# The edge between two rounds of a chunked RWKV-7 scan, written in another order on four queues

## The chip, the cores and the metric

The kernel runs on one core of one Trainium2 chip. The metric is the device time of one execution in microseconds (us), the median of several. A core has a matrix engine (TensorE, PE in the profile; its weight loads are PEld), a vector engine (VectorE, DVE), an activation engine (ScalarE, ACT), GpSimd (POOL) and SyncE (SP), which issues the transfers. Each works through its own queue in order and waits on semaphores for the others.

## The reference

Two encoder layers over 512 tokens of width 1024. Each mixes tokens in two groups side by side, latent attention and a bidirectional RWKV-7 scan of 8 heads, projects the result out, and ends in a gated MLP with a convolution. The change concerns the RWKV group alone:

```python
h = rms_norm(x) * (1 + sc1) + sh1
z_rwkv = centred_token_shift((h @ w_in[l])[..., MLA_IN:], rwkv_mu[l])
def step(state, inp):                      # wkv7_scan: 512 tokens, forward and reversed
    sa = jnp.einsum('bhvk,bhk->bhv', state, -kk_t)
    state = (state * w_t[:, :, None, :] + sa[..., None] * (kk_t * a_t)[:, :, None, :]
             + v_t[..., None] * k_t[:, :, None, :])
    y = jnp.einsum('bhvk,bhk->bhv', state, r_t)
...
y = y_f + y_b                              # rwkv7_group: 8 heads of 64
y = ((y - mu) * lax.rsqrt(var + GN_EPS)).reshape(B, S, W) * gn_g + gn_b
return (y + bonus.reshape(B, S, W)) * g
...
x = x + gt1 * (jnp.concatenate([y_mla, y_rwkv], axis=-1) @ w_out[l])
x = x + gt2 * conv_ffn(rms_norm(x) * (1 + sc2) + sh2, ...)
```

## The kernel before

**Stages.** A layer runs the input projection, the latent attention, the RWKV stage, the output projection, and the MLP. In the profiled execution the RWKV stage of the first layer stands at about 285 to 558 us and that of the second at about 1251 to 1535 us. This stage uses hardly any transfers.

**Blocks and rounds.** RW is 512 channels, or four blocks of 128 (two heads `e` each), and both directions `d` are worked on together. The 512 tokens of a block are cut into 8 chunks of 64. `rwkv_round(l, cur, nxt)` is called for `cur` = -1, 0, 1, 2, 3 (PE line 801). In one round the engines scan block `cur` in eight steps `s`, build what block `nxt = cur + 1` needs, and finish block `cur - 1` (`trail`). Round -1 only builds; round 3 only scans and finishes. What a reader sees as "the edge" is the stretch between the last step of one round and the first solve of the next.

**One step of the scan.** `scan_state` (L614, L618, L620) multiplies by the carried state, `scan_solve` (L627) multiplies by the inverse of the chunk's triangle, `scan_update` (L637 for the next state, L643 for the output) closes the step. Between them stand the products for later chunks: `scan_gram` for `s + 2` (L577), `scan_values` for `s + 1` (L599) and the transposes `scan_tokens` for `s + 2` (L589, L591, L592). VectorE masks each Gram pair into one of two buffers `GR` (L1419, "the mask") and scales the state (L1425, "the state product"). ScalarE moves R (L975), the token transposes (L970) and the solution (L982) out of the banks. A step can't begin its solve before the state product of the step before it.

**The build of the next block.** VectorE sums the decays (L1283), makes the queries of a direction (L1290 to L1296), its removals (L1301, L1304) and its keys (L1309, L1311); these need ScalarE's exponentials `grown` (Pp, L917) and `shrunk` (Pi, L921) and the factor f (L926). TensorE makes the triangles (L524), ScalarE moves them (L938), VectorE transposes them into lanes (`inverse_in`, L1342) and inverts them by rows of 8, 16 and 32 (L1348 to L1406), then transposes the result back (`inverse_out`, L1414, "out"). The bonus is made by L1315, L1317, a product on TensorE (L532) and L1322.

**The level.** At the edge TensorE turns the 32 by 32 inverses into 64 by 64 ones: 32 transposes X (L543), 32 products T (L548) and 32 products Z (L556). ScalarE evicts each half (L952, L957, L964) and copies the two diagonals (`diagonal`, L945, two operations each). After the level TensorE issues Gram pair 1, values 0 and tokens 1, and then the first solve. Before the level stand the early products of the block after next (`rwkv_early`, L509, in banks 5 and 6), with ScalarE's `early_decay` and `early_rate` (L905, L907, L912) and a reversed copy of the values (L931), and Gram pair 0 and tokens 0.

**The tail of a block.** ScalarE takes the output of the scan (L989), TensorE centres it at step 3 (L650) and sums its squares at step 5 (L655), ScalarE takes a logarithm and an exponential, each with a table load (L999, L1001), TensorE multiplies by the gate (L657), and VectorE finishes the norm (`tail_norm`, L1432 to L1436) at step 6.

**What sets the order.** The order on each queue is the order of the calls in the `rwkv_round` of that engine (PE, ACT and DVE have one each), written by hand. `at(name, round)` and `before(name, round)` turn the name of a step into the count of a semaphore.

## Time and profile before

| | us |
|---|---|
| three timed runs | 1986.78, 1987.35, 1992.8 |
| their median | 1987.35 |
| the profiled execution's own time | 1992.84 |
| its span | 1990.9 |
| PE busy | 1706.3 (86%) |
| DVE busy | 1072.9 (54%) |
| ACT busy | 720.6 (36%) |
| POOL busy | 292.1 (15%) |

The profiled execution lies at the upper end of the three timed runs; 1.94 us of it lie outside the span. Over the whole span TensorE is busy 86% of the time, but this is an average over dense projections and the RWKV stage, where the four queues wait for each other in turn. Rows of the timeline give start, duration, engine, line, operation and operands, and in square brackets the idle time of that engine just before and what ended it.

### The profile page before, as it was taken

To read this page: it belongs to the slowest core of one execution; us is meant where nothing else is said; L and a number is where in the kernel's file an instruction comes from. 1 tells how busy PE (TensorE), PEld (TensorE's weight loads), DVE (VectorE), ACT (ScalarE), POOL (GpSimd) and SP (SyncE) were. 2 spreads that over 40 slices of the span, in tenths; PEclk is the share of its full clock that TensorE was granted. 3 is DMA by queue.
4 is the path that set the end of the run, shared out by engine and by line. 5 is a ranking of instruction groups with operands and counts; after the bars stand their busy time and mean duration, and the time that the engine had idled before them with its cause. 6 is when DMAs were issued, how large, how long until landed. Compare 5 with 4: busy or idle time off the path is not lost.

```text
span 1990.9 us, 27789 instructions
## 1 busy us (share of the span) xinstructions
PE 1706.3 (86%) x11192; PEld 1262.2 (63%) x11192; DVE 1072.9 (54%) x1533; ACT 720.6 (36%) x1160; POOL 292.1 (15%) x124
## 2 busy tenths in 40 slices
PE   2996855888877999999989988488888989999997
PEld 1783424656654888878858734266665668888785
DVE  6744558777344767663343343876773155454433
ACT  3433243445424232322243343434544232322322
POOL 0440000000022121211124400000000212221220
PEclk8998875788788999999999989576777989999999
DMA  7443110000032555542303300000001212223222
GB/s 275 169 158 112 43 59 1 2 2 2 2 144 89 187 192 180 199 148 85 116 23 117 108 29 1 0 2 2 1 2 43 85 64 86 104 84 105 85 87 82
DMA packets 34651, 162.96 MB, mean 82 GB/s; under 512 B 3840, under 2 KB 4096, under 8 KB 25856
## 3 DMA queue, kind: packets, MB, share of 16 engines
q1 hardware_dynamic: 34560, 161.65, 23.3%
q8 instruction: 69, 1.13, 0.2%
q14 instruction: 22, 0.18, 0.0%
HBM read 159.54 MB, written 2.10 MB: 81 GB/s over the span
## 4 chain that ended last, share of the span: by engine, by line
PE 71%; DVE 17%; ACT 6%; issue 5%; DMA 1%; POOL 0%; DVEq 0%; SPq 0%; ACTq 0%; POOLq 0%
PE bank L487 12%; PE bank L489 12%; PE bank L488 12%; PE bank_pair L487 4%; PE bank_pair L489 4%; PE bank_pair L488 4%; DVE work L1336 3%; PE bank L774 2%; PE bank L775 2%; PE bank L556 1%; PE bank_pair L577 1%; PE bank L548 1%; DVE work L1395 1%; PE bank L752 1%; PE bank L704 1%
## 5 line engine op out<-in xcount | busy, mean ns | idle before, releaser
L487 PE MATMUL bank<-work_parts,y_mix_parts 128*128 128x512 f32 x792 | 316.1, 399 | 24.3 <-DVE work_parts L1499 16.0
L489 PE MATMUL bank<-work_parts 128*128 128x512 f32 x792 | 314.9, 398 | 0.0
L1512 DVE TENSOR_TENSOR work_parts<-work,y_mix_parts 128x1024 fp32r<-128x1024 f32 x66 | 169.4, 2567 | 253.5 <-ACT y_mix_parts L876 253.5
L1721 POOL TENSOR_TENSOR proj_weights_parts<-proj_weights,proj_weights_hi 128x1024 fp32r<-128x1024 f32 x54 | 131.5, 2438 | 1049.8 <-ACT proj_weights_hi L870 974.1
L1726 POOL TENSOR_TENSOR work_parts<-work,y_mix_parts 128x1024 fp32r<-128x1024 f32 x66 | 160.4, 2431 | 616.8 <-ACT y_mix_parts L876 616.8
L876 ACT ACTIVATE y_mix_parts<-work 128x1024 fp32r<-128x1024 f32 x132 | 132.8, 1054 | 251.3 <-DMA work<-mlp_dram 251.3
L488 PE MATMUL bank<-work_parts,y_mix_parts 128*128 128x512 f32 x528 | 209.0, 396 | 0.0
L487 PEld LDWEIGHTS bank<-work_parts,y_mix_parts 128*128 128x128 f32 x792 | 150.2, 190 | 66.3 <-issue 24.8
L489 PEld LDWEIGHTS bank<-work_parts 128*128 128x128 f32 x792 | 150.2, 190 | 35.6
L487 PE MATMUL bank<-work_parts,proj_weights_hi 128*128 128x512 f32 x304 | 126.5, 416 | 42.1 <-DVE work_parts L1499 27.0
L489 PE MATMUL bank<-work_parts,proj_weights_parts 128*128 128x512 f32 x304 | 123.5, 406 | 0.0
L488 PEld LDWEIGHTS bank<-work_parts,y_mix_parts 128*128 128x128 f32 x528 | 100.1, 190 | 23.2
L488 PE MATMUL bank<-mixer_inputs_parts,y_mix_parts 128*128 (+1 forms) x264 | 104.5, 396 | 0.0
L489 PE MATMUL bank_pair<-work_parts 128*128 128x512 f32 x264 | 104.4, 396 | 0.0
L487 PE MATMUL bank_pair<-work_parts,y_mix_parts 128*128 128x512 f32 x264 | 104.2, 395 | 0.0
L487 PEld LDWEIGHTS bank<-work_parts,proj_weights_hi 128*128 128x128 f32 x304 | 60.1, 198 | 65.6 <-issue 36.1
L577 PE MATMUL bank_pair<-work 64*128 64x128 f32 x512 | 62.2, 349 | 31.0 <-DVE work L1419 30.4
L1215 DVE CUSTOM_DVE_ANT_0 work<-work,c_act 128x1024 f32<-128x1024 f32 x64 | 80.5, 1295 | 12.3 <-DMA work<-ada_dram 12.2
L1172 ACT ACTIVATE work<-work 128x512 f32<-128x512 f32 x44 | 27.9, 633 | 160.3 <-DVE work L1669 160.3
L488 PE MATMUL bank<-work_parts,proj_weights_hi 128*128 128x512 f32 x208 | 83.0, 399 | 0.0
L577 PEld LDWEIGHTS bank_pair<-work 64*128 64x128 f32 x512 | 47.6, 231 | 40.6 <-DVE work L1419 35.5
L509 PE MATMUL bank<-mixer_inputs 64*128 64x512 f32 x64 | 40.8, 1035 | 33.6 <-DVE y_mix L1322 13.1
(253 smaller groups left out, 3176.2 us busy)
## 6 DMA issues: line engine op xcount, KB each, us to landing
work<-mlp_dram SPq DMA_DIRECT2D x66, 1024.0 KB, 4.9
work<-ada_dram SPq DMA_DIRECT2D x64, 512.0 KB, 4.6
proj_weights<-tiles_dram SPq DMA_DIRECT2D x57, 512.0 KB, 3.5
x_res<-ada_dram SPq DMA_DIRECT2D x24, 512.0 KB, 4.9
x_res<-x_dram SPq DMA_DIRECT2D x2, 2048.0 KB, 10.6
mixer_inputs<-ada_dram SPq DMA_DIRECT2D x8, 512.0 KB, 17.5
work<-mlaw_dram SPq DMA_DIRECT2D x4, 640.0 KB, 4.3
out_dram<-x_res SPq DMA_DIRECT2D x8, 256.0 KB, 2.2
```

What stands on the lines that cost most here:

```text
L487: mm(out, w_hi, x_hi, start=start, stop=False)
L488: mm(out, w_hi, x_lo, start=False, stop=False)
L489: return mm(out, w_lo, x_hi, start=False, stop=stop)
L509: own(ear_p, mm(PS[5 + d][:, :], l_rw[rows, b, i, :], mix(x)[rows, :], start=True, stop=True), f"{n}{d}")
L577: last = mm(PS[3 + e][:, d * P:(d + 1) * P], BK[p][d][rows, s, :, :], ZR[p][d][rows, s, :, :], start=True, stop=True)
L774: mm(bank[:, :], QN[:, e, qb * P:(qb + 1) * P], KN[:, e, :], start=True, stop=False)
L876: F(MW_H[q][:, half], MW_IN[q][:, half], ACT.Identity).then_inc(msp_a.sem, msp_a.one(f"h{half}"))
L1215: dve.tensor_tensor_reduce(out=slots[u], in0=slots[u], in1=CACT, scale=0.5, scalar=0.0, op0=ALU.mult, op1=ALU.add, accum_out=dots[:, u:u + ...
L1336: return TTT(tmp, rows.unsqueeze(1).to_broadcast([64, c, a, j]), cols.unsqueeze(2).to_broadcast([64, c, a, j]), ALU.mult)
L1512: TTT(MW_L[q][:, 1], MW_IN[q][:, 1], plain(MW_H[q][:, 1]), ALU.subtract).then_inc(msp_v.sem, msp_v.one("l1"))
L1721: pool.tensor_tensor(ring_l[s], ring[s], plain(ring_h[s]), ALU.subtract).then_inc(spl_q.sem, spl_q.one(f"t{s}"))
L1726: pool.tensor_tensor(MW_L[q][:, 0], MW_IN[q][:, 0], plain(MW_H[q][:, 0]), ALU.subtract).then_inc(msp_q.sem, msp_q.one("l0"))
```

## The change

All of it is in the RWKV stage; the work is the same except where named.

- **Edge, TensorE.** Gram pair 1 goes between the transposes X and the products T, values 0 and tokens 1 between T and Z; before, all three stood behind Z. Early products and level use banks 1 and 2 in place of 5 and 6. Since bank 2 holds the output of the scan, the early products now wait until ScalarE has taken it, and until the last solution is evicted.
- **Edge, ScalarE.** The exponentials stand between the evictions of the level: Pp0 and Pp1 before the evictions of T0 and T1, Pi0 behind them, Pi1 between Z0 and Z1. Before, Pp1 and Pi1 stood behind the level. Half of the diagonal copies go to VectorE. Both factors f follow the first solve. The reversed copy of the values moves from the edge to step 4.
- **Edge, VectorE.** Queries and removals of both directions, two diagonal copies and the norm of the block two rounds back stand ahead of step 0. In the steps, each mask comes first; behind it the two key pairs at step 0, the bonus at 1, the inverse in other portions at 2 to 7.
- **Tail.** The gate product moves from step 5 to behind step 6, and the norm to the edge of the next round; in round 3 its own norm stays at step 6. The norm works in YQ.
- **Masks.** `GR` has three buffers in place of two, and a mask waits for its Gram pair only, not for the tokens behind it.

```diff
-        GR = [view(WORK, 8192 + 512 * p, 2, 2, P) for p in range(2)]
+        GR = [view(WORK, 8192, 2, 2, P), view(WORK, 8704, 2, 2, P), view(RS, 512, 2, 2, P)]
...
-                elif trail:
-                    pe.wait_ge(tl_v.sem, tl_v.at("gt", it - 3))
-                else:
-                    pe.wait_ge(tri_a.sem, tri_a.at("B11", it - 1))
-                    pe.wait_ge(bon_v.sem, bon_v.at("bon", it - 1))
+                if scan:
+                    pe.wait_ge(sc_a.sem, sc_a.at(f"SA{NCH - 1}", it - 2))
+                    pe.wait_ge(tl_a.sem, tl_a.at("y", it - 2))
...
-                        own(ear_p, mm(PS[5 + d][:, :], l_rw[rows, b, i, :], mix(x)[rows, :], start=True, stop=True), f"{n}{d}")
+                        own(ear_p, mm(PS[1 + d][:, :], l_rw[rows, b, i, :], mix(x)[rows, :], start=True, stop=True), f"{n}{d}")
...
-                if d == 0:
-                    pe.wait_ge(lev_a.sem, lev_a.before("Z1", it))
-                    pe.wait_ge(ear_a.sem, ear_a.at("A1", it))
+                if d == 0 and it % RB >= 3:
+                    pe.wait_ge(tl_v.sem, tl_v.at("gt", it - 3))
...
                 if early:
                     pe.wait_ge(ear_a.sem, ear_a.at("A1", it + 1))
-                else:
-                    pe.wait_ge(tl_v.sem, tl_v.at("gt", it - 2))
+                elif scan:
+                    pe.wait_ge(sc_a.sem, sc_a.at(f"SA{NCH - 1}", it - 1))
+                    pe.wait_ge(tl_a.sem, tl_a.at("y", it - 1))
...
                     own(lev_p, last, f"X{d}")
+                scan_gram(it, 1)
                 for d in D2:
...
                     own(lev_p, last, f"T{d}")
+                scan_values(it, 0)
+                scan_tokens(it, b, 1)
                 pe.wait_ge(lev_a.sem, lev_a.at("T1", it))
...
+                if s == 0:
+                    pe.wait_ge(inv_v.sem, inv_v.at("d1", it))
...
+                    if trail and s == 6:
+                        tail_gate(old, cur - 1)
...
-                for e in range(2):
-                    src = XD[32 * q:32 * q + 32].rearrange("p (d e c) t -> p e d c t", d=2, e=2)[:, e]
-                    own(lev_a, F(XT[it % 2][64 * e + 32 * q:64 * e + 32 * q + 32, :, :, 32 * q:32 * q + 32], src, ACT.Identity), f"D{q}{e}")
+                src = XD[32 * q:32 * q + 32].rearrange("p (d e c) t -> p e d c t", d=2, e=2)[:, 1]
+                own(lev_a, F(XT[it % 2][64 + 32 * q:96 + 32 * q, :, :, 32 * q:32 * q + 32], src, ACT.Identity), f"D{q}")
...
                     act.wait_ge(lev_p.sem, lev_p.at(f"X{d}", it))
-                    own(lev_a, F(X0T[0:32, 16 * d:16 * d + 16, :], sixteen(PS[5 + d][0:32, :]), ACT.Identity), f"X{d}")
-                if nxt < RB:
-                    grown(it + 1, 0)
+                    own(lev_a, F(X0T[0:32, 16 * d:16 * d + 16, :], sixteen(PS[1 + d][0:32, :]), ACT.Identity), f"X{d}")
                 for d in D2:
+                    if nxt < RB:
+                        grown(it + 1, d)
                     act.wait_ge(lev_p.sem, lev_p.at(f"T{d}", it))
-                    own(lev_a, F(X0T[32:64, 16 * d:16 * d + 16, :], sixteen(PS[5 + d][32:64, :]), ACT.Identity), f"T{d}")
+                    own(lev_a, F(X0T[32:64, 16 * d:16 * d + 16, :], sixteen(PS[1 + d][32:64, :]), ACT.Identity), f"T{d}")
...
-                    own(lev_a, F(XT[it % 2][rows, :, :, 32:64], PS[5 + e][rows, :].rearrange("p (d c t) -> p d c t", d=2, c=NCH), ACT.Identity), f"Z{e}")
+                    own(lev_a, F(XT[it % 2][rows, :, :, 32:64], PS[1 + e][rows, :].rearrange("p (d c t) -> p d c t", d=2, c=NCH), ACT.Identity), f"Z{e}")
+                    if e == 0 and nxt < RB:
+                        shrunk(it + 1, 1)
                 diagonal(it, 1)
...
-                act.wait_ge(tl_v.sem, tl_v.before("gt", it))
+                act.wait_ge(tl_p.sem, tl_p.before("cen", it))
...
-                if scan:
-                    scan_state(it, 0)
-                elif build:
-                    grown(new, 0)
-                    shrunk(new, 0)
-                if build:
-                    grown(new, 1)
-                    shrunk(new, 1)
+                if build and not scan:
+                    for d in D2:
+                        grown(new, d)
+                    for d in D2:
+                        shrunk(new, d)
                 for s in range(NCH):
                     if scan:
-                        if s:
-                            scan_state(it, s)
+                        scan_state(it, s)
                         if s < NCH - 1:
                             scan_ring(it, s + 1)
                         scan_solve(it, s)
+                    if build and s == 0:
+                        factor(new, nxt, 0)
+                        factor(new, nxt, 1)
                     if build and s in (0, 1):
-                        factor(new, nxt, s)
                         triangle(new, s)
+                    if build and scan and s == 4:
+                        backward_values(new, nxt)
                     if trail and s == 3:
                         tail_square(old)
...
-                    backward_values(new + 1, nxt + 1)
...
+            def diagonal(it, q):
+
+                dve.wait_ge(inv_v.sem, inv_v.at("out", it))
+                src = XD[32 * q:32 * q + 32].rearrange("p (d e c) t -> p e d c t", d=2, e=2)[:, 0]
+                own(inv_v, dve.tensor_copy(XT[it % 2][32 * q:32 * q + 32, :, :, 32 * q:32 * q + 32], src), f"d{q}")
...
-                dve.wait_ge(sc_p.sem, sc_p.at(f"K{s}" if s > 1 else f"G{s}", it))
-                own(sc_v, TTT(GR[s % 2].rearrange("p e d x -> p e (d x)"), PAIR[:, :, 0:256], gmask.unsqueeze(1).to_broadcast([P, 2, 256]), ALU.mult),
+                dve.wait_ge(sc_p.sem, sc_p.at(f"G{s}", it))
+                own(sc_v, TTT(GR[s % 3].rearrange("p e d x -> p e (d x)"), PAIR[:, :, 0:256], gmask.unsqueeze(1).to_broadcast([P, 2, 256]), ALU.mult),
...
                     queries(new, nxt, 0)
+                if scan:
+                    diagonal(it, 0)
+                    diagonal(it, 1)
+                if build:
+                    queries(new, nxt, 1)
                     removals(new, nxt, 0)
+                    removals(new, nxt, 1)
+                if cur > 1:
+                    tail_norm(old - 1, cur - 2)
                 for s in range(NCH):
-                    if build:
-                        if s == 0:
-                            queries(new, nxt, 1)
-                        if s == 1:
-                            keys(new, nxt, 0)
-                        if s == 2:
-                            bonus(new, nxt)
-                        if s == 3:
-                            inverse_8(new, 1, 7)
-                        if s == 4:
-                            bonus_end(new, nxt)
-                            inverse_16_second(new)
-                        if s == 5:
-                            inverse_32_first(new, 0)
-                        if s == 6:
-                            inverse_32_mid(new, 1)
                     if scan and s < NCH - 1:
                         scan_ring(it, s + 1)
                     if build:
                         if s == 0:
-                            removals(new, nxt, 1)
+                            keys(new, nxt, 0)
+                            keys(new, nxt, 1)
                         if s == 1:
-                            keys(new, nxt, 1)
+                            bonus(new, nxt)
                         if s == 2:
                             inverse_in(new)
+                            inverse_8(new, 1, 4)
                         if s == 3:
-                            inverse_8(new, 7, 8)
+                            inverse_8(new, 4, 8)
                             inverse_16_first(new)
                         if s == 4:
+                            bonus_end(new, nxt)
+                            inverse_16_second(new)
                             inverse_16_end(new)
                         if s == 5:
+                            inverse_32_first(new, 0)
                             inverse_32_first(new, 1)
+                        if s == 6:
                             inverse_32_mid(new, 0)
-                        if s == 6:
-                            inverse_32_second(new, 0)
-                    if trail and s == 6:
+                            inverse_32_mid(new, 1)
+                    if trail and not build and s == 6:
                         tail_norm(old, cur - 1)
                     if scan and s < NCH - 1:
                         scan_state(it, s)
                     if build and s == 7:
+                        inverse_32_second(new, 0)
                         inverse_32_second(new, 1)
```

**ScalarE at the edge** between the rounds 0 and 1 (L952/L959 evict X, L957/L964 evict T, L964/L971 evict Z, L945/L952 copy a diagonal, L917/L924 is Pp, L921/L929 is Pi, L975/L984 takes R; before, then now):

```order
L970 ACTIVATE work<-bank 128x512
L952 ACTIVATE work<-bank 32x512 x2
L917 ACTIVATE work<-work 128x512
L957 ACTIVATE work<-bank 32x512 x2
L921 ACTIVATE work<-work 128x512
L945 ACTIVATE work<-work 32x16x32 x2
L964 ACTIVATE work<-bank 32x16x32 x2
L945 ACTIVATE work<-work 32x16x32 x2
L975 ACTIVATE rstd<-bank 128x128
L917 ACTIVATE work<-work 128x512
L921 ACTIVATE work<-work 128x512
```

```order
L979 ACTIVATE work<-bank 128x512
L959 ACTIVATE work<-bank 32x512 x2
L924 ACTIVATE work<-work 128x512
L964 ACTIVATE work<-bank 32x512
L924 ACTIVATE work<-work 128x512
L964 ACTIVATE work<-bank 32x512
L929 ACTIVATE work<-work 128x512
L952 ACTIVATE work<-work 32x16x32
L971 ACTIVATE work<-bank 32x16x32
L929 ACTIVATE work<-work 128x512
L971 ACTIVATE work<-bank 32x16x32
L952 ACTIVATE work<-work 32x16x32
```

The second Pp moved from behind the R eviction into the gap of the T products, the second Pi into the gap of the Z products, and each diagonal is one copy in place of two.

**VectorE at the steps 2 and 3** of a round, from one state product to the next but one (L1419/L1433 is the mask, L1425/L1439 the state product, L1342/L1350 `inverse_in`, L1348 to L1365 the rows up to 8 and the first product of 16, L1356 to L1373 now; before, then now):

```order
L1419 TENSOR_TENSOR work<-bank_pair,constants 128x512
L1342 STREAM_TRANSPOSE work<-work 64x1024
L1425 TENSOR_TENSOR rstd<-bank,chunk_ends 128x128
L1348 COPY lane_inverse<-work 64x4
L1354 TENSOR_TENSOR work<-work,lane_inverse 64x16
...
L1356 TENSOR_REDUCE lane_inverse<-work 64x4x6
L1419 TENSOR_TENSOR work<-bank_pair,constants 128x512
L1354 TENSOR_TENSOR work<-work,lane_inverse 64x196
L1356 TENSOR_REDUCE lane_inverse<-work 64x4x7
L1336 TENSOR_TENSOR work<-work,lane_inverse 64x512 x2
L1365 TENSOR_REDUCE work<-work 64x128
L1425 TENSOR_TENSOR rstd<-bank,chunk_ends 128x128
```

```order
L1433 TENSOR_TENSOR work<-bank_pair,constants 128x512
L1350 STREAM_TRANSPOSE work<-work 64x1024
L1356 COPY lane_inverse<-work 64x4
L1362 TENSOR_TENSOR work<-work,lane_inverse 64x16
L1364 TENSOR_REDUCE lane_inverse<-work 64x4x2
L1362 TENSOR_TENSOR work<-work,lane_inverse 64x36
L1364 TENSOR_REDUCE lane_inverse<-work 64x4x3
L1439 TENSOR_TENSOR rstd<-bank,chunk_ends 128x128
L1433 TENSOR_TENSOR work<-bank_pair,constants 128x512
L1362 TENSOR_TENSOR work<-work,lane_inverse 64x64
...
L1373 TENSOR_REDUCE work<-work 64x128
L1439 TENSOR_TENSOR rstd<-bank,chunk_ends 128x128
```

The rows 1 to 3 of the inverse moved ahead of the state product of step 2, and the mask of step 3 moved from behind row 6 to right behind that state product.

**TensorE at the same edge** (L543/L542 is X, L548 is T, L556/L558 is Z, L577/L579 a Gram pair, L599/L601 values, L589 to L592 and now L591 to L594 tokens, L627/L631 the solve; before, then now):

```order
L543 MATMUL bank<-constants,work 32x32 x32
L548 MATMUL bank<-work 32x32 x32
L556 MATMUL bank<-work 32x32 x32
L577 MATMUL bank_pair<-work 128x128 x4
L599 MATMUL bank<-work 64x64 x4
L589 MATMUL bank<-constants,work 128x128 x2
L591 MATMUL bank<-constants,mixer_inputs 128x128
L592 MATMUL bank<-constants,work 128x128
L627 MATMUL bank<-rstd,work 64x64 x4
```

```order
L542 MATMUL bank<-constants,work 32x32 x32
L579 MATMUL bank_pair<-work 128x128 x4
L548 MATMUL bank<-work 32x32 x32
L601 MATMUL bank<-work 64x64 x4
L591 MATMUL bank<-constants,work 128x128 x2
L593 MATMUL bank<-constants,mixer_inputs 128x128
L594 MATMUL bank<-constants,work 128x128
L558 MATMUL bank<-work 32x32 x32
L631 MATMUL bank<-rstd,work 64x64 x4
```

The Gram pair moved ahead of T and the values and tokens ahead of Z, so that the solve follows Z directly.

## Rows read from the trace of the kernel before

**Rows 1.** Windows: length; busy PE, PEld, DVE, ACT, POOL; clock share; six building scans, then one level.

```profile
342.55:379.92 37.37, 29.20 (x551) 23.55 (x550) 32.43 (x56) 13.03 (x36) 0.00 (x0) 0.91 0.01 2
401.14:442.39 41.25, 33.35 (x557) 25.05 (x557) 34.20 (x59) 17.30 (x41) 0.00 (x0) 0.87 0.01 2
460.11:500.94 40.83, 33.10 (x558) 24.98 (x557) 34.29 (x59) 17.29 (x41) 0.00 (x0) 0.88 0.01 2
1308.96:1349.07 40.11, 32.84 (x552) 25.92 (x551) 32.50 (x56) 13.03 (x36) 0.00 (x0) 0.80 0.01 2
1371.48:1412.29 40.81, 33.08 (x557) 24.96 (x556) 34.28 (x59) 17.29 (x41) 0.00 (x0) 0.88 0.01 2
1434.71:1474.07 39.36, 31.62 (x558) 24.01 (x557) 34.43 (x59) 17.29 (x41) 0.00 (x0) 0.93 0.01 2
330.26:342.55 12.29, 11.61 (x180) 10.65 (x181) 5.45 (x9) 7.86 (x14) 0.00 (x0) 0.50 0.01 1
```

**Rows 2.** Timeline of round 2, all engines, steps 0 to 4.

```profile
460.27 0.68 DVE L1290 TENSOR_TENSOR work<-mixer_inputs,work 128x504 f32<-128x504 f32 x1 [4.95 <-ACT work L917]
461.59 0.80 ACT L926 ACTIVATE work<-work,derived 128x512 f32<-128x512 f32 x1
468.50 0.45 PE L627 MATMUL bank<-rstd,work 64*64 64x64 f32 x8 [0.33 <-ACT rstd L975]
473.41 0.45 PE L627 MATMUL bank<-rstd,work 64*64 64x64 f32 x8 [0.32 <-ACT rstd L975]
473.81 1.96 DVE L1342 STREAM_TRANSPOSE work<-work 64x1024 f32<-64x1024 f32 x1
476.89 0.22 DVE L1354 TENSOR_TENSOR work<-work,lane_inverse 64x64 f32<-64x64 f32 x1
479.24 0.82 PE L577 MATMUL bank_pair<-work 64*128 64x128 f32 x8 [1.73 <-DVE work L1419]
482.33 0.27 DVE L1425 TENSOR_TENSOR rstd<-bank,chunk_ends 128x128 f32<-128x128 f32 x1
483.82 0.69 DVE L1322 TENSOR_TENSOR y_mix<-bank,mixer_inputs 128x512 f32<-128x512 f32 x1 [1.22 <-PE bank L532]
488.13 0.27 DVE L1425 TENSOR_TENSOR rstd<-bank,chunk_ends 128x128 f32<-128x128 f32 x1
```

**Rows 3.** One line of the trace, L1395: durations in ns, smallest, median, largest.

```profile
L1395 DVE TENSOR_REDUCE work<-work x16: 1197/1738/2280, 317.8 to 1467.6; 64x128 f32<-64x2048 f32 x8, 64x128 f32<-64x1024 f32 x8
```

**Rows 4.** Timeline of round 3, its last steps in the first layer.

```profile
538.58 0.45 PE L627 MATMUL bank<-rstd,work 64*64 64x64 f32 x8
542.75 1.12 PE L657 MATMUL bank<-mixer_inputs 128*128 128x512 f32 x2 [0.78 <-ACT squares L999]
544.74 0.75 DVE L1432 SCALAR_TENSOR_TENSOR squares<-bank,params,squares 128x512 f32<-128x512 f32 x1 [2.90 <-ACT squares L1001]
544.85 0.45 PE L627 MATMUL bank<-rstd,work 64*64 64x64 f32 x8
546.92 0.28 DVE L1425 TENSOR_TENSOR rstd<-bank,chunk_ends 128x128 f32<-128x128 f32 x1
```

**Rows 5.** Timeline of the first level: T, Z, Gram pair 1, second diagonal, R.

```profile
332.07 3.62 PE L548 MATMUL bank<-work 32*32 32x32 f32 x64
336.37 3.43 PE L556 MATMUL bank<-work 32*32 32x32 f32 x64 [0.68 <-ACT work L957]
339.72 0.93 PEld L577 LDWEIGHTS bank_pair<-work 64*128 64x128 f32 x8
340.44 1.28 ACT L945 ACTIVATE work<-work 32x512 f32<-32x512 f32 x2
341.75 0.28 ACT L975 ACTIVATE rstd<-bank 128x128 f32<-128x128 f32 x1
```

**Rows 6.** Timeline at the end of round 1: ScalarE takes the output of the scan.

```profile
443.99 0.60 ACT L989 ACTIVATE squares<-bank 128x512 f32<-128x512 f32 x1 [0.55 <-PE bank L643]
```

**Rows 7.** Timeline of the one level that TensorE began at the full clock.

```profile
450.75 2.50 PE L548 MATMUL bank<-work 32*32 32x32 f32 x64 [0.21 <-ACT work L952]
```

59 lines of the change are left out of this document (30 added, 29 removed).

## Prediction

> **What bounds the kernel now.** I read three views in this order: busy time in windows cut at the first and last solve of each scan, the timeline of one round and of one level on all engines, and a single line's durations. The windows say which engine is near its limit. In the six scans that carry a build (rounds 0, 1 and 2 of each layer) VectorE is busy 32.4 to 34.4 us out of 37.4 to 41.3, TensorE 29.2 to 33.4, ScalarE 13.0 to 17.3 [rows 1]. None is full; the queues wait for each other in turn. The six windows add up to 37.37 + 41.25 + 40.83 + 40.11 + 40.81 + 39.36 = 239.7 us. In the level TensorE is busy 11.61 of 12.29 us, but its granted clock is 0.50, the 1.2 GHz level, all through, and VectorE is busy only 5.45 [rows 1].
>
> The timeline shows VectorE's two troubles. At the edge it idles 4.95 us until the second Pp, which stands on ScalarE behind the whole level (460.27, [rows 2]); what it could not do there it does in the steps. And in step 3 TensorE waits 1.73 us for a mask that VectorE has queued behind six rows of the inverse (479.24, [rows 2]). So within the steps VectorE, or a wait on it, comes last; at the edge TensorE does. The change works on both.
>
> **The scans.** A step is priced from solve to solve. I lay VectorE's new queue end to end from one state product to the next and ask whether TensorE or ScalarE is later. Between a state product and the next operation VectorE needs 0.2 us, for a mask 0.6.
>
> Step 0: the Gram pair no longer waits for a mask behind the queries, but both key pairs now stand ahead of the state product. They follow f, and f follows the solution's eviction on ScalarE, 1.3 us after the solve: two f of 0.80 end at 2.9, the last two of four key operations of about 0.7 at 4.8, and then comes the state product. On TensorE it makes little difference: the wait for the mask, 460.11 to about 462.3 in this round, becomes 0.6, so that triangle 0 ends about 1.6 us sooner and ScalarE moves it and takes R 1.6 us sooner. 468.50 - 460.11 = 8.39 becomes 6.85 [rows 1, 2]. Step 1: bound by triangle 1 and its move, as before, 473.41 - 468.50 = 4.91 [rows 2]. Step 2: `inverse_in` can start when the triangle is moved, without the mask in front of it (0.6 saved), and rows 1 to 3 of the inverse (1.0) are added ahead of the state product: 473.81 to 476.89 less the 0.2 of the state product is 2.9, which puts the next solve 8.99 after the solve of step 1 and leaves 4.08 for step 2 [rows 2]. Step 3: from row 4 of the inverse to the state product 482.33 - 476.89 = 5.44, mask included, and 0.2: 5.64 [rows 2]. The bonus and the centring on TensorE end within that. Step 4: 488.13 - 482.33 = 5.80, less the 1.22 us for which VectorE waited for the bonus product, which is done earlier now: 4.58 [rows 2]. Steps 5 and 6 of round 0: 0.2 + 0.6 + a large and a small operation of the inverse. The reduction of 2048 columns takes 2.28 and of 1024 columns 1.20 [rows 3]; with starts overlapping a little 3.33, so 4.13 for either step. In rounds 1 and 2 ScalarE comes last at step 5: logarithm and exponential, each with a table load, stand ahead of R. Round 3, where VectorE has nothing else, shows this chain alone, 544.85 - 538.58 = 6.27 [rows 4]. At step 6 the gate product (1.12, [rows 4]) is on TensorE's path: 3.65.
>
> Round 0: 6.85 + 4.91 + 4.08 + 5.64 + 4.58 + 4.13 + 4.13 = 34.3. Round 1: 6.85 + 4.91 + 4.08 + 5.64 + 4.58 + 6.27 + 3.65 = 36.0. Round 2: 0.8 more, since the norm of block 0 holds up the first mask: 36.8. Two layers: 214.2. **Gain 239.7 - 214.2 = 25.5 us.**
>
> **What the change costs.** (a) *The level.* TensorE's work is the same, in another order, and its clock stays at half, so moving a product saves nothing by itself. Before, Gram pair, values and tokens ran from 339.72 to 342.55, behind Z; they covered ScalarE's eviction of Z, both diagonals and R [rows 1, 5]. Now the solve waits for that bare: Z ends at 336.37 + 3.43 = 339.80, the diagonals start at 340.44, one takes 0.64, R 0.28 and its hand-over 0.1, together 1.6. Against it stands the wait of 0.68 between T and Z, which the products now fill [rows 5]. 12.29 - 0.68 + 1.6 = 13.2 with roundings 13.1: +0.8, eight levels, 6.4 us. (b) *The early products* wait until the output is taken, 0.60 [rows 6] and a hand-over of 0.1, where they now start beside it; they lead to the level in two edges per layer: 4 x 0.7 = 2.8. (c) *The edge of round 2 to 3* has no early products. It starts when the inverse is out, and one operation of the inverse more stands behind the last state product: 2 x 0.45 = 0.9. (d) *Round -1*: the queries of direction 1 (two of 0.68, as at 460.27 in [rows 2]; two small copies lie in the overlap) go ahead of the first removals, on which triangle 0 waits, and nothing scans beside it: 1.35 x 2 = 2.7. (e) *Round 3*: its norm still stands ahead of the state product of step 6, but the gate that it waits for now comes behind `scan_update(6)`. The gate, which began at 542.75, can't begin before about 546.5, 1.6 us behind the solve of 544.85, and takes 1.12; the norm starts at 547.65 rather than 544.74 [rows 4] and the state product, 546.92 before, follows at 549.8: +2.9, twice, 5.8. Together 18.6.
>
> Costed at nothing: the two diagonal copies and the norm on VectorE (about 1.2 and 2.2 us), because VectorE is free for 12.29 - 5.45 = 6.8 us of a level [rows 1]; were that cover gone they would cost 3.4 in the rounds that have both. The reversed copy of the values (about 0.6) stands at step 4 of ScalarE, which is busy for less than half of any scan [rows 1]. Nothing moves on SP's or POOL's queue.
>
> **Sum:** 25.5 - 18.6 = 6.9 us less. The profiled execution's own 1992.84 would become 1985.9; against the median of 1987.35 that is 1980.5.
>
> **The bounds.** The least known term is step 0, since it depends on when the full clock comes. In the windows the clock's mean is between 0.80 and 0.93 [rows 1], so the half clock reaches over 5 to 16 us in some of them. Step 0 between 6.1 (full clock) and 7.7 (triangle at half clock) makes the six gains differ by -5 to +5. Term (a) lies between 0.3 (if R is taken while Z still runs) and 1.3: 4 us either way.
>
> The Trainium skill, page "TensorE: Matmul & The Clock Gate", Part 1, says that "the default state is throttled, and activity releases the throttle". By that sentence a level busy for 11.61 of 12.29 us should not sit at 0.50, so the trace speaks against the plain reading. By that rule products of full size in the middle of the level might release the clock; the mechanism is the last rival below, with its price from rows.
>
> **The rivals.**
>
> *The edge stays at full clock until the level.* Between the last solve and the level stand the early products, a Gram pair and tokens. If the denser end of a scan keeps the clock up there, they shrink as T does, 3.62 to 2.50 [rows 5, 7], by 0.3 of their length: of some 8 us, as I estimate the stretch, 2.5. Three edges with that: another 7, about 1973. For it: the steps 5 and 6 lose their waits for VectorE. Against it: a mean clock of 0.80 to 0.93 shows that the scans' products did not hold the clock throughout [rows 1].
>
> *The steps are not shortened as much.* ScalarE or TensorE is close behind VectorE in steps 1, 3 and 5, so perhaps only three quarters of the 25.5 come, while the costs, all of them plain serial waits, come in full: 19.1 - 18.6, or 1987.
>
> *Slower: the scan starts at half clock and stays there for two steps.* Before, the dense products from 339.72 on stood right ahead of the first solve [rows 5]; now thin products and 1.6 us of idling do. If the full clock then comes after step 1 rather than in step 0, each of six rounds loses about 0.8 us on triangle 0 and 1.7 on the step behind it, and each of the two last rounds 1.7: about 18, so 6.9 less becomes 11 more: 1998. It decides when the half clock lasts more than about 4 us longer into the scan than now. The windows' means show that it now lasts into step 0 in most rounds.
>
> *The order is executed but the waits stay.* If VectorE still idles at the queries for the second Pp, because that stands behind the eviction of T0, up to 2 us per round are left: 12 us lost of 25.5. I count it with the second rival.
>
> *The level runs at full clock.* The one block of T products that began at full clock took 2.50 us in place of 3.62 [rows 5, 7]. A level shortened in that ratio, 13.1 to about 9.6 with ScalarE's share kept, eight times: another 28, 1952. Against it: the level of [rows 1] sat at 0.50 although TensorE was busy for all but 0.7 us of it.
>
> **How the numbers follow.** About 0.3%, or 6 us, is what a measurement of this kernel can tell from no change. Forecast (1974 to 1988) 0.58, of which 0.38 fall below 1981.4; warm edges 0.14, faster; steps less shortened 0.16, nearly all within 0.3%; slower by the clock 0.08; level at full clock 0.04. That makes faster 0.56, same 0.34, slower 0.10. The predicted time is the forecast's, 1980.5. The range leaves out the last two cases: 1969 to 1990.
>
> **What the profile would show.** Right: the solves of a building round 34 to 37 us from first to last; no wait for a mask at the Gram pair of step 3; a level of 13 us at half clock with TensorE idle for 1.5 us before the solve; VectorE's idle 4.95 gone; in round 3 the last step from solve to solve 6 us in place of 3.2. Wrong: a first step of 8 us or more at half clock; a VectorE that reaches the first mask after the solve in rounds 0 and 1; a step 5 above 6.5.

## The result, and the profile after

| | before | after |
|---|---|---|
| median of the timed runs, us | 1987.35 (5 runs, 1985.93 to 1992.8) | 1999.84 (5 runs, 1998.61 to 2004.39) |
| ratio to before | 1 | 1.0054 (95%: 1.0038 to 1.007) |
| profiled execution: own time, span | 1992.84, 1990.9 | 2000.57, 1998.6 |

The changed kernel is slower by 0.5%. The forecast was 1980.5 with a range of 1969 to 1990, and faster: wrong in sign, and outside the range.

I cut both traces at the same marks of the RWKV stage, to see where the difference lies. Each number is the sum over both layers, in us, from the starts of the first and the last solve of each scan.

| stretch | before | after | difference | predicted |
|---|---|---|---|---|
| six building scans | 239.73 | 220.61 | -19.1 | -25.5 |
| six edges between rounds | 121.79 | 132.69 | +10.9 | +8.5 |
| round 3, twice | 57.53 | 69.68 | +12.2 | +5.8 |
| round -1 and first level (from the norm ahead of the stage), twice | 137.26 | 141.62 | +4.4 | +4.3 |
| last solve to the projection's first eviction, twice | 17.52 | 20.26 | +2.7 | 0 |
| RWKV stage | | | +11.0 | -6.9 |
| everything else | | | -3.3 | 0 |

"Everything else" is mostly a prologue that was 5.5 us shorter in this execution (first mark at 264.9 us, before at 270.5). The change does not touch it, and the runs of before spread by as much. So the stage, not the span, is what the steps are held against.

The windows of after that answer to [rows 1]: length; busy PE, PEld, DVE, ACT, POOL; clock share. Three building scans and round 3 of the first layer, round 3 of the second, then the last level of the first layer.

```profile
339.22:373.93 34.71, 28.83 (x551) 23.11 (x551) 27.74 (x48) 13.05 (x35) 0.00 (x0) 0.92 0.01 2
397.62:433.98 36.36, 31.41 (x556) 23.91 (x556) 28.66 (x49) 17.43 (x40) 0.00 (x0) 0.93 0.01 2
457.19:496.15 38.96, 33.27 (x556) 25.25 (x556) 30.91 (x52) 17.42 (x40) 0.00 (x0) 0.87 0.01 2
515.88:552.15 36.27, 31.66 (x426) 23.94 (x427) 7.72 (x16) 13.37 (x33) 0.00 (x0) 0.78 0.01 2
1495.61:1529.02 33.41, 28.66 (x426) 21.94 (x426) 7.72 (x16) 13.37 (x33) 0.00 (x0) 0.91 0.01 2
502.64:515.88 13.24, 11.61 (x180) 10.65 (x180) 4.02 (x7) 5.10 (x10) 0.00 (x0) 0.50 0.00 1
```

VectorE is busy 2.9 to 5.6 us less per building scan than in [rows 1] (32.43 to 27.74, 34.20 to 28.66 and 34.29 to 30.91 in the first layer): what was moved to the edge left the steps. The scans of rounds 0 and 1 are 34.7 and 36.4 us, as forecast (34.3 and 36.0). Round 2 is 38.96 where 36.8 was forecast. Round 3 had no build to shorten; the same window of before shows what it lost in length and in clock:

```profile
520.03:548.08 28.05, 26.31 (x427) 20.04 (x427) 8.29 (x16) 13.55 (x33) 0.00 (x0) 0.99 0.01 3
```

The end of round 3 in after, timeline, against [rows 4]:

```profile
540.67 1.02 PE L660 MATMUL bank<-squares,constants 128*128 128x512 f32 x2
542.43 1.28 ACT L1010 ACT_TABLE_LOAD   x1
544.58 0.45 PE L631 MATMUL bank<-rstd,work 64*64 64x64 f32 x8 [1.85 <-ACT rstd L984]
546.45 2.08 PE L665 MATMUL bank<-mixer_inputs 128*128 128x512 f32 x2
548.57 0.75 DVE L1446 SCALAR_TENSOR_TENSOR squares<-bank,params,squares 128x512 f32<-128x512 f32 x1 [7.62 <-PE bank L665]
550.74 0.28 DVE L1439 TENSOR_TENSOR rstd<-bank,chunk_ends 128x128 f32<-128x128 f32 x1
552.15 0.69 PE L631 MATMUL bank<-rstd,work 64*64 64x64 f32 x8
```

This is the centre of the case. In step 5 R waits behind ScalarE's logarithm, table load and exponential. Before, TensorE worked through the gate product in that wait (542.75, [rows 4]); now it stands idle for 1.85 us. Then the granted clock falls to 1.2 GHz: the gate product, issued at 546.45, takes 2.08 us where it took 1.12, and the norm and the state product queue behind it. The last step from solve to solve is 7.57 us, 3.23 before. Round 2 has the same idle and the same fall; the windows give the granted clock of the end of step 5 and of step 6, 1.00 and 0.64:

```profile
491.37 0.67 PE L631 MATMUL bank<-rstd,work 64*64 64x64 f32 x8 [1.85 <-ACT rstd L984]
493.74 1.66 PE L665 MATMUL bank<-mixer_inputs 128*128 128x512 f32 x2
...
488.42:491.37 2.95, 1.10 (x19) 0.84 (x18) 2.95 (x3) 2.81 (x5) 0.00 (x0) 1.00 0.00 0
491.37:496.15 4.78, 4.61 (x50) 2.97 (x50) 3.41 (x4) 1.26 (x4) 0.00 (x0) 0.64 0.01 3
```

The fall does not always come. Of six such idles of 1.85 us (rounds 1, 2 and 3 of two layers) three are followed by it: in round 2 of both layers and in round 3 of the first layer.

### The profile page after: what moved, and what is told of

Its sections match the earlier page's. It is cut to its first block, busy times and chain, and to the rows that moved or that the text cites. A ratio compares the mean times of both kernels' runs of the same rounds, so it can differ in the third digit from the quotient of the medians.

```text
span 1998.6 us, 27794 instructions
## 1 busy us (share of the span) xinstructions
PE 1711.6 (86%) x11192; PEld 1264.0 (63%) x11192; DVE 1078.8 (54%) x1549; ACT 712.7 (36%) x1144; POOL 291.3 (15%) x124
## 3 DMA queue, kind: packets, MB, share of 16 engines
q8 instruction: 69, 1.13, 0.2%
## 4 chain that ended last, share of the span: by engine, by line
PE 74%; DVE 14%; ACT 6%; issue 5%; DMA 1%; POOL 0%; DVEq 0%; SPq 0%; ACTq 0%; POOLq 0%
PE bank L488 12%; PE bank L490 12%; PE bank L489 12%; PE bank_pair L488 4%; PE bank_pair L490 4%; PE bank_pair L489 4%; DVE work L1344 2%; PE bank_pair L579 2%; PE bank L780 2%; PE bank L781 1%; PE bank L548 1%; PE bank L758 1%; PE bank L508 1%; PE bank L710 1%; PE bank L558 1%
## 5 line engine op out<-in xcount | busy, mean ns | idle before, releaser
L488 PE MATMUL bank_pair<-work_parts,y_mix_parts 128*128 128x512 f32 x264 | 104.4, 395 | 0.0
L489 PE MATMUL bank_pair<-work_parts,y_mix_parts 128*128 128x512 f32 x176 | 69.1, 393 | 0.0
L490 PEld LDWEIGHTS bank<-work_parts,proj_weights_parts 128*128 128x128 f32 x304 | 59.5, 196 | 14.4
L877 ACT ACTIVATE proj_weights_hi<-proj_weights 128x1024 fp32r<-128x1024 f32 x30 | 31.6, 1056 | 99.6 <-DMA proj_weights<-tiles_dram 99.6
```

Of the source, the lines that this page charges most:

```text
L488: mm(out, w_hi, x_hi, start=start, stop=False)
L489: mm(out, w_hi, x_lo, start=False, stop=False)
L490: return mm(out, w_lo, x_hi, start=False, stop=stop)
L877: F(ring_h[t % 3], ring[t % 3], ACT.Identity).then_inc(spl_a.sem, spl_a.one(f"t{t % 3}"))
```

## The experiments

Two theories came out of the traces. **Gate theory:** the gate product left a place where it was free for one where it is on TensorE's path, and its old place is now an idle stretch after which the clock falls. **Level theory** (close to the "slower" rival of the prediction): with the dense products moved away from the first solve, step 0 runs more of its length at half clock than it would with them in place. A third possibility was that all of the loss lies in the waits that the edge gained, and that the clock has nothing to do with it. All ratios are to the kernel before, measured beside it on the same chip. "Rounds, total" below is first solve to last solve, both layers of the profiled execution: 419.1 before, 423.0 after. Each profile is one execution, and 29 runs of the kernel before lay between 1983.15 and 1995.85 us, so a difference of 2 or 3 us between two totals is not told from chance.

### The gate product back at step 5

```diff
                         tail_variance(old)
-                    if trail and s == 6:
                         tail_gate(old, cur - 1)
```

> The changed kernel with the gate product back at step 5, behind the sum of squares. Theory G (the move of the gate is what turned the gain into a loss): at step 5 the gate ran while ScalarE loaded its table and took the exponential, so it cost nothing there and kept TensorE busy; behind step 6 it stands on the path. Step 6 of round 1 falls from 3.60 to 2.5 in both layers; step 6 of round 3 from 7.57 and 6.22 to about 3.2, since the norm need not wait for the gate; the half clock at the end of round 3 goes (tail of the first layer 10.15 to 7.9). Together 10 to 14 us, near 1987. Theory L (the level is the loss, the gate is a side issue): only the waits of round 3 go, 2 x 2.9, so 1994.

Measured: 1985.53 (12 runs), ratio 0.9976 (0.996 to 0.9991); rounds, total 408.4. Timeline of round 3, then windows of round 2 and round 3:

```profile
540.43 1.28 ACT L1009 ACT_TABLE_LOAD   x1
540.46 1.12 PE L665 MATMUL bank<-mixer_inputs 128*128 128x512 f32 x2 [0.78 <-ACT squares L1007]
542.57 0.45 PE L631 MATMUL bank<-rstd,work 64*64 64x64 f32 x8
...
458.33:494.32 35.99, 31.06 (x556) 23.55 (x557) 29.34 (x51) 17.44 (x40) 0.00 (x0) 0.93 0.01 3
515.59:545.79 30.20, 28.46 (x426) 21.82 (x426) 7.72 (x16) 13.39 (x33) 0.00 (x0) 0.91 0.01 2
```

The product runs under the table load again, at full clock. Round 3 is 6.1 us shorter in the first layer and 3.2 in the second, round 2 3.0 and 3.7; the edges are 2.8 longer in all. Of the expectation, step 6 of round 1 came to 2.77 (2.5 expected), the last step of round 3 to 3.22 (3.2), but the tail of the first layer only to 9.22 (7.9). This one edit turns the change from a loss of 0.54% into a gain of 0.24%: moving the gate product cost about 0.8%, or 15 us, enough to reverse the sign.

### A filler in the gate's old place

The changed kernel with two more products of 256 columns behind the sum of squares of step 5, into free columns of a bank; the gate stays at step 6. The filler makes no result of its own, but what is added up later in that bank is no longer the reference's, so only its time is read.

```diff
                         tail_variance(old)
+                        for _ in range(2):
+                            mm(PS[0][:, 256:512], ident, CST[:, K_SCAN:K_SCAN + 256], start=True, stop=True)
```

> The changed kernel with two more products of 256 columns at step 5, behind the sum of squares, into a part of a bank that nothing reads; the gate stays behind step 6. This puts work in the gap of 1.85 us that TensorE has there, without taking anything off step 6. Theory C (the clock: the gap at step 5 is what lets it fall at the end of rounds 2 and 3): the granted clock stays at full through steps 6 and 7 of these rounds; step 6 of round 2 falls from 4.78 and 5.48 to 3.6, that of round 3 from 7.57 to about 6.2, the tail of the first layer from 10.15 to 7.9: 5 to 7 us, near 1994. Theory P (the path alone matters, the clock follows something else): no change, 1999 to 2000.

Measured: 1996.01 (12 runs), ratio 1.002 (1.0007 to 1.0033); rounds, total 420.6. Timeline of round 2, then the window of round 3:

```profile
490.99 1.03 PE L696 MATMUL bank<-constants 128*128 128x256 f32 x4
494.04 0.45 PE L631 MATMUL bank<-rstd,work 64*64 64x64 f32 x8 [0.99 <-ACT rstd L986]
495.75 1.13 PE L665 MATMUL bank<-mixer_inputs 128*128 128x512 f32 x2
518.10:550.88 32.78, 29.03 (x430) 22.46 (x430) 7.72 (x16) 13.36 (x33) 0.00 (x0) 0.92 0.01 2
```

Work that nobody needs makes the kernel 0.3% faster than the changed one: in round 2 the clock holds through step 6, the gate product takes 1.13 again, step 6 of round 2 is 3.60 in place of 4.78 and 5.48, and the last step of round 3 is 6.46 in both layers (without the filler 7.57 with the fall and 6.22 without it). The tail of the first layer, expected at 7.9, stayed at 10.15. This separates the gate's cost roughly into two parts. What the filler brings back (0.34% of 0.78%) is clock; the other half is the product and the norm on the path, with the clock that is lost while TensorE waits 2.55 us for that norm (round 3 at 549.8: the product behind it takes 0.69 in place of 0.45).

### Round 3's norm behind the state product

```diff
-                    if trail and not build and s == 6:
-                        tail_norm(old, cur - 1)
                     if scan and s < NCH - 1:
                         scan_state(it, s)
+                    if trail and not build and s == 6:
+                        tail_norm(old, cur - 1)
```

> The changed kernel with one edit: in round 3 VectorE's norm stands behind the state product of step 6 in place of ahead of it. Only the wait of the norm for the gate product is taken off the path: step 6 of round 3 falls from 7.57 and 6.22 to 3.6 by my sum (4.8 if the gate still runs at half clock), so 5 to 7 us less than the changed kernel, of which 2.9 a layer is the wait and the rest the clock. If the gate product itself is the loss and not the norm's wait for it, the step stays above 5.

Measured: 1993.91 (12 runs), ratio 1.0016 (0.9998 to 1.0033). Timeline of round 3 in the second layer:

```profile
1521.40 0.29 DVE L1439 TENSOR_TENSOR rstd<-bank,chunk_ends 128x128 f32<-128x128 f32 x1 [5.24 <-PE bank L641]
1521.52 1.13 PE L665 MATMUL bank<-mixer_inputs 128*128 128x512 f32 x2
1522.68 0.75 DVE L1446 SCALAR_TENSOR_TENSOR squares<-bank,params,squares 128x512 f32<-128x512 f32 x1 [0.99 <-PE bank L665]
```

The state product no longer waits for gate and norm. The last step falls from 7.57 and 6.22 to 4.80 and 3.60, 5.4 us together, and the whole by about 0.4% (ratios 1.0054 and 1.0016). Term (e) of the prediction had the right mechanism. The clock still falls behind the idle of step 5: 4.80 in one layer, and step 6 of round 2 is 5.09 and 5.48. In this execution it also fell in round 1 of the first layer (5.48 in place of 3.60), which the edit doesn't touch: which idles are followed by a fall changes from one execution to the next.

### The level in its old order

Gram pair 1, values 0 and tokens 1 behind Z again; all else as changed.

```diff
                     own(lev_p, last, f"X{d}")
-                scan_gram(it, 1)
...
                     own(lev_p, last, f"T{d}")
-                scan_values(it, 0)
-                scan_tokens(it, b, 1)
...
                     own(lev_p, last, f"Z{e}")
+                scan_gram(it, 1)
+                scan_values(it, 0)
+                scan_tokens(it, b, 1)
```

> The changed kernel with Gram pair 1, values 0 and tokens 1 behind the Z products again, as before the change; all else is the changed kernel. Theory L (the waits for the last eviction, the diagonal and R stand bare before the solve, and dense products ahead of the solve bring the full clock back sooner): each level 0.8 to 0.9 shorter, eight times 7, and the first step 0.5 to 1 shorter in some rounds, together 7 to 12, 1988 to 1993. Theory N (the level's order doesn't matter, since the products are on the path either way): within 2 us of 2000.

Measured: 1984.14 (12 runs), ratio 0.9959 (0.9943 to 0.9975); rounds, total 407.3. Windows: the last level of the first layer from its first transpose to the solve, then step 0 of round 2; for comparison step 0 of round 2 in after.

```profile
501.77:514.06 12.29, 11.61 (x180) 10.65 (x180) 4.10 (x7) 5.06 (x9) 0.00 (x0) 0.50 0.01 1
459.12:465.31 6.19, 4.85 (x127) 4.03 (x126) 4.38 (x8) 4.27 (x9) 0.00 (x0) 0.94 0.01 3
```

```profile
457.19:465.71 8.52, 7.26 (x127) 6.05 (x127) 6.35 (x11) 3.79 (x9) 0.00 (x0) 0.59 0.01 2
```

The level is 0.95 us shorter than the 13.24 of after, near term (a). The larger part is what comes behind it: step 0 is 6.20 in five of six building scans (6.83 in the sixth), where after has 7.1 to 8.5, and in round 2 of the first layer its mean clock is 0.94 in place of 0.59. In all, the six building scans are 10.9 us shorter, the edges 2.6, round 3 2.2. Of the 10.9, step 0 gives 7.8. The other 3.1 are step 6 of round 2, 3.60 in both layers: the idle of 1.85 us stands there as before, and the clock held. In round 3 it fell behind that idle in both layers (7.56 and 7.68).

### A filler behind Z

The changed kernel with three products of 256 columns behind Z, ahead of the first solve. Nobody reads them.

```diff
                     own(lev_p, last, f"Z{e}")
+                pe.wait_ge(lev_a.sem, lev_a.at("Z0", it))
+                for _ in range(3):
+                    mm(PS[1][:, 256:512], ident, CST[:, K_SCAN:K_SCAN + 256], start=True, stop=True)
```

> The changed kernel, the level in its new order, with three products of 256 columns added behind Z, in the 1.5 us that TensorE idles before the solve; they write columns that nothing reads and are no part of the computation. Theory C (dense work right ahead of the solve brings the full clock back sooner, which is most of what level_old won): step 0 falls from 7.1 to 7.5 towards the 6.2 of level_old although the level is no shorter, 3 to 6 us less than the changed kernel. Theory W (level_old won by a shorter chain alone): step 0 stays above 7 and the time is that of the changed kernel or a little over.

Measured: 1998.24 (12 runs), ratio 1.0038 (1.0022 to 1.0053). Timeline and window of round 2:

```profile
458.85 2.93 PE L563 MATMUL bank<-constants 128*128 128x256 f32 x6
461.71 0.69 PE L634 MATMUL bank<-rstd,work 64*64 64x64 f32 x8
461.71:467.91 6.20, 5.44 (x128) 4.51 (x127) 4.36 (x8) 3.67 (x8) 0.00 (x0) 0.84 0.01 3
```

Step 0 is 6.10 to 6.20 in all six scans, so it was the clock, not a wait, that made it long, and products ahead of the solve bring the clock back. But at half clock they took 2.93 us against an idle of 1.63, so the six edges grew by 0.6 to 1.4 us each, 7.1 in all, which took back most of the 8.9 that the building scans gained. Rounds, total, are 418.2; the ratio lies 0.16% under that of the changed kernel, and their intervals overlap, so this run shows where the clock goes and not a faster kernel. The old order does the same with products that are needed anyway.

All eight kernels with the steps in the changed order bear the level theory out. With the new order of the level and no filler (24 building scans in four kernels) step 0 takes 6.86 to 8.58 us; with the old order (18 scans in three, the next two sections included) 6.20 to 6.83 but for one of 8.00; with this filler 6.10 to 6.20. The exception stands behind a level that TensorE began at the full clock and that itself took 10.64 us in place of 12.29.

### Both parts back, and the mask ring alone

The gate at step 5 and the level in its old order, together (both diffs above):

> Both edits together: the gate product at step 5 and the level in its old order, all else the changed kernel. If the two losses are separate (theory G and theory L each right), the gains add: against the kernel before, gate5 was 0.24% and level_old 0.41% faster, the changed kernel 0.54% slower, so 0.24 + 0.41 + 0.54 = 1.19% faster than before, a ratio of 0.988. If they are one loss seen twice (both through the clock at the first step), the ratio stays at 0.994 to 0.996.

Measured: 1969.35 (6 runs), ratio 0.9892 (0.9867 to 0.9917). Rounds, total 395.5: 27.5 us under after, where the single edits gave 14.5 and 15.7. They add up nearly in full, and the ratio is near the 0.988 expected for two separate losses. The windows of round 2's step 0 and of round 3:

```profile
453.40:459.64 6.24, 5.95 (x128) 4.99 (x127) 4.44 (x8) 3.95 (x9) 0.00 (x0) 0.75 0.01 3
508.39:537.35 28.96, 27.22 (x428) 20.86 (x427) 7.73 (x16) 13.53 (x33) 0.00 (x0) 0.95 0.01 3
```

The kernel before with the ring of three masks alone: a mask waits for its Gram pair and comes first in each step.

```diff
-        GR = [view(WORK, 8192 + 512 * p, 2, 2, P) for p in range(2)]
+        GR = [view(WORK, 8192, 2, 2, P), view(WORK, 8704, 2, 2, P), view(RS, 512, 2, 2, P)]
...
-                dve.wait_ge(sc_p.sem, sc_p.at(f"K{s}" if s > 1 else f"G{s}", it))
+                dve.wait_ge(sc_p.sem, sc_p.at(f"G{s}", it))
...
+                    if scan and s < NCH - 1:
+                        scan_ring(it, s + 1)
                     if build:
                         if s == 0:
...
-                    if scan and s < NCH - 1:
-                        scan_ring(it, s + 1)
```

> The kernel before with one part of the change alone: three mask buffers, a mask waits for its Gram pair only, and each mask is the first operation of VectorE in its step. All other order is that of before. Theory M (the masks queued behind the inverse are most of what the steps lost): step 3 falls from 8.5 to about 6.3, step 0 from 8.4 to 6.9 where the first mask no longer stands behind the queries; two to three us in each of six rounds, 12 to 18 us, 1970 to 1975. Rival V (VectorE's sum of work sets the round, the masks only move the wait): the gain of a step is given back at the end of the inverse, under 4 us, 1984 to 1987.

Measured: 1976.73 (6 runs), ratio 0.9924 (0.9902 to 0.9945). A small part of the change, alone, does better than the change: the building scans are 17.3 us shorter in all (19.1 in the changed kernel), and round 3 costs nothing (56.6 against 57.5 us for both). The edges are 5.9 longer, most of it (4.4) the one between rounds 1 and 2 of the first layer, which in before began its level at the full clock. Rounds, total, are 406.8. Step 3 took 6.8 us in five of six scans, where 6.3 was expected.

### A version that beats both

Gate and level as above, the norm behind the state product in round 3, and the early products of direction 0 no longer wait for the output to be taken; those of direction 1 still do, since the output is in their bank.

```diff
                     pe.wait_ge(sc_a.sem, sc_a.at(f"SA{NCH - 1}", it - 2))
-                    pe.wait_ge(tl_a.sem, tl_a.at("y", it - 2))
...
                             pe.wait_ge(ear_a.sem, ear_a.at(f"W{d}", it))
+                        elif d == 1 and scan:
+                            pe.wait_ge(tl_a.sem, tl_a.at("y", it - 2))
```

> gate5_level_old with two more edits: in round 3 VectorE's norm stands behind the state product of step 6, and the early products of direction 0, which write bank 1, no longer wait until ScalarE has taken the output from bank 2. Expected against gate5_level_old: step 6 of round 3 stays at 3.2 (the norm waits for nothing there, it may fall to 2.8), the edges from round 0 and 1 shorter by 0.6 if the wait for the output was what the early products lost, by nothing if TensorE's half clock sets the stretch. In all 1 to 3 us, a ratio of 0.986 to 0.988.

Measured: 1966.95 (6 runs, 1958.33 to 1970.53), ratio 0.9879 (0.9851 to 0.9908). It is faster than before by 1.2%; whether it is faster than the version with gate and level alone (0.9892) these runs don't tell. Its profiled execution (1960.32) is among its fastest; rounds, total, are 388.8. The edges between rounds 0 and 1, at half clock in both kernels, are 0.8 us shorter than with gate and level alone: that is what the wait for the output cost, 0.7 by term (b). Windows of round 1 and round 3:

```profile
394.06:428.69 34.63, 30.09 (x558) 22.70 (x557) 27.83 (x48) 17.70 (x40) 0.00 (x0) 0.98 0.01 3
504.21:531.87 27.66, 26.38 (x427) 20.11 (x427) 6.47 (x15) 13.53 (x33) 0.00 (x0) 0.99 0.01 3
```

## Why the prediction was wrong, point by point

**Steps 1 to 5 of the building scans: right.** Forecast 4.91, 4.08, 5.64, 4.58, then 4.13 or 6.27; measured 4.91, 4.23, 5.76, 4.48, 4.14 and 6.27, and within 0.03 of that in the other five scans (step 5: 6.27 where ScalarE comes last). Laying VectorE's queue end to end, with durations of before, gave the steps to 0.15 us. The wait for a mask ([rows 2], 1.73) and VectorE's 4.95 us at the edge are gone; its idle stretches there are now 1.06, 0.92 and 1.79.

**Step 0: mis-sized.** 6.85 was forecast, bounded by 6.1 and 7.7, and 0.8 more in round 2, where the norm of block 0 was to hold up the first mask. Measured: 7.28, 7.11, 8.52 and 7.22, 7.06, 8.48, in all 3.0 us over the forecast. In round 2 this is over 8 us, which the prediction had named as a sign of being wrong. The norm is not the cause: with the old level and with the filler it stands in the same place, and step 0 of round 2 is 6.20, but for one of 6.83. The same two runs show the cost of the clock to be 0.9 to 1.1 in rounds 0 and 1 and 1.6 to 2.3 in round 2.

This is near the "slower" rival, which had chance 0.08, but not the rival as written. It let the full clock come after step 1 rather than in step 0. In all six building scans of after, step 1 is 4.91 at a clock of 1.00; only in round 3 of the first layer did the half clock reach into step 1 (0.64). Before, with the dense products in place, four of six scans had step 0 at 0.60 to 0.64 as well, so half clock doesn't reach further than it did in those. That the rival's 1998 lies near the measured 1999.84 is luck: 18 us were to come from steps 0 and 1 alone, and much of the loss came from the gate.

**Step 6: the size right, the clock missed.** 3.65 with the gate on the path: measured 3.60 in round 1, but 4.78 and 5.48 in round 2, 3.0 us over the forecast. The fault lies one step earlier. I priced the gate product where it went, and not the hole it left. The old place was free: it lay under ScalarE's table load. Its departure left TensorE idle for 1.85 us, and the runs show that this idle, not the product, lost the clock. In the four kernels that have it (after, the norm moved, the old level, the filler behind Z) 13 of 24 such idles are followed by a gate product of 1.66 to 2.08 us. In the four where the gate product or the filler fills the place, the product took 1.12 to 1.13 all 24 times.

**Term (e), round 3: mechanism right, size 5.8 against 12.2.** In the second layer, where the clock held, the last step is 6.22 in place of 3.23, so +3.0 against the 2.9 forecast, and the norm behind the state product takes most of that away. The sum had nothing for the clock: +1.35 on the last step of the first layer (7.57), and in steps 0 and 1, at half clock, +2.3 and +1.5 in the first layer (6.07 and 5.03, against 3.73 and 3.49) and +0.9 in the second. 2 x 3.0 + 1.35 + 4.7 is the 12.2 of the table, within roundings.

**Terms (a) and (d), the level and round -1: right.** The last level is 13.24 against 13.1 forecast, at 0.50, with 1.63 us idle before the solve; round -1 with the first level cost 4.4 against 4.3.

**Terms (b) and (c), the edges: (b) near, (c) not seen, and the clock missed.** In the second layer the edges grew by 1.31, 0.83 and 0.16, against 1.5, 1.5 and 1.25. In the first layer they grew by 2.47, 5.49 and 0.64. The third of each layer grew by less than its level alone, so the 0.45 of (c) doesn't show. Before, the second edge of the first layer had a mean clock of 0.78, and its level began at full clock ([rows 7]); after, no edge is above 0.64, and all levels run at 0.50:

```profile
442.39:460.11 17.72, 15.02 (x216) 11.57 (x217) 12.13 (x13) 13.77 (x25) 0.00 (x0) 0.78 0.00 1
```

```profile
433.98:457.19 23.21, 19.37 (x216) 14.90 (x216) 17.32 (x23) 13.21 (x24) 0.00 (x0) 0.56 0.00 1
```

So the "warm edges" were a thing to lose rather than to gain. What makes an edge warm stays open: the version that beats both has edges between rounds 1 and 2 of 18.77 and 19.44 us, at 0.81 and 0.76, while with the mask ring alone the same edges take 22.2 and 22.4.

**The tail: missed.** From the last solve to the projection's first eviction 2.3 us more in the first layer, at half clock (0.50; before 1.00), 0.5 in the second (0.50; before 0.59). I priced the scans and levels and not what runs behind them at the same clock.

**The others.** The diagonal copies and the norm on VectorE stayed hidden. "The waits stay" and "the level runs at full clock" did not happen in the changed kernel.

In short, the gains came to three quarters, and the costs, forecast as plain serial waits, grew from 18.6 to 30.1 us. The step that failed is that the sum had no term for what the new order does to TensorE's clock. The stage came out 17.9 us worse than forecast: 3.0 in step 0, 3.0 in step 6 of round 2, 6.4 in round 3, 2.4 at the edges and 2.7 in the tail, the rest in the other steps. Each of these stretches ran at half clock, wholly or in part. The fillers show the cost for step 0 and step 6 of round 2 and for round 3 (its step 0 is 4.70 and 4.55 behind the filler at Z, in place of 6.07, and step 1 of the first layer 3.49 in place of 5.03); for the edges and the tail it is read from the granted clock alone.

## What to carry to other kernels

Price a moved instruction in the place that it leaves as well as where it goes: work under another engine's wait is free there, and on a clock-gated engine it also pays for what runs behind it. Keep the dense products directly ahead of the step whose speed matters, and fill an unavoidable wait with needed work, since filler that runs at half clock gives most of its gain back. When one part of a large reordering carries most of the benefit, as the masks with their third buffer did here (0.76% alone, of 1.2% in the best version), try it alone before the rest.

## What the runs showed of the hardware

An idle of 1.85 us in the middle of a busy scan was followed by a fall of the granted clock from 2.4 to 1.2 GHz three times out of six, and 13 times out of 24 over four kernels. Rounds 1 and 2 have the same TensorE instructions around it. In round 1 of the first layer the clock held, and the gate product took 1.12 us as before:

```profile
430.38 0.45 PE L631 MATMUL bank<-rstd,work 64*64 64x64 f32 x8 [1.85 <-ACT rstd L984]
432.10 1.12 PE L665 MATMUL bank<-mixer_inputs 128*128 128x512 f32 x2
```

Why one round keeps its clock and the next loses it was not settled.

A level of 32 by 32 products doesn't bring the full clock back: 77 of the 80 levels of these ten profiles ran at 0.50 or 0.51, although TensorE is busy for 11.61 of 12.29 us (the level in its old order above). In the other three TensorE still had the full clock at the start and lost it within the level (10.67 us at 0.64 in before, 10.64 at 0.66 and 11.31 at 0.59 in the version that beats both). The Trainium skill, page "TensorE: Matmul & The Clock Gate", Part 1, says that activity releases the throttle. These levels don't bear that out by busy time alone, while the products of 256 columns behind Z do agree with it, since step 0 behind them fell from 8.52 to 6.20 us.
